# Scan of a hybrid decoder layer: the first group's sums ahead of the inverse's first step, the gate ahead of the state's sum, the output scale on ScalarE, constants as bias of logarithms

## The reference, cut to what matters

```
# SSD branch, per chunk, 4 groups of 8 heads
y = (decay * C B^T * dt) x  +  (C h) * exp(acum)          # inside the chunk + from the state
h = h * exp(last) + (w x)^T B                             # state
y = rmsnorm_per_group((y + D x) * silu(z)) * w            # gate, then a norm per group
# delta-rule branch, per chunk, 8 heads
u, w = (I + A)^-1 [beta v, beta k exp(g)]                 # triangular solve
v_new = u - w S;  o = q S + attn v_new;  S = S exp(last) + k^T v_new
o = rmsnorm(o) * w * silu(gate)
# q and k are l2-normalised: q * rsqrt(sum(q*q) + EPS), and the norms add EPS too
```

## Time and profile before

| what | us |
|---|---|
| median of 3 runs (3299.76 to 3300.80) | 3299.77 |
| the profiled execution | 3298.78 |
| its span in the profile | 3296.9 |
| PE busy, whole span | 2961.9 (90%) |
| DVE busy | 1542.7 (47%) |
| ACT busy | 1008.8 (31%) |
| POOL busy | 387.1 (12%) |

### The profile page before, as it was taken

The page is one execution under the profiler, slowest core; times in us unless marked ns, Lnnn a source line. Parts: engine busy times, 40 slices in busy tenths (PEclk is TensorE's granted clock), DMA queues, the critical chain, the costliest instruction groups (busy, mean ns, idle before and its releaser), DMA issues. The chain is left out here.

```text
span 3296.9 us, 52404 instructions
## 1 busy us (share of the span) xinstructions
PE 2961.9 (90%) x18908; PEld 2803.8 (85%) x18908; DVE 1542.7 (47%) x2327; ACT 1008.8 (31%) x2050; POOL 387.1 (12%) x540
## 2 busy tenths in 40 slices
PE   3799999999999888888888785999879999997998
PEld 2799999999999876777777634999879999997998
DVE  5355555521111177777778654455453323233443
ACT  2222222221121153444444334333341212122332
POOL 2000000000000033222223211000110000000100
PEclk7899999999999999899989886999999999998999
DMA  2222222222242213342222636564531122215443
GB/s 77 80 93 92 91 91 91 91 99 94 93 133 94 94 24 77 86 90 64 64 64 66 168 106 256 176 206 158 171 99 65 58 78 83 78 58 188 169 143 112
DMA packets 238754, 348.18 MB, mean 106 GB/s; under 512 B 154520, under 2 KB 173288, under 8 KB 238368
## 3 DMA queue, kind: packets, MB, share of 16 engines
q1 hardware_dynamic: 233264, 325.20, 31.2%
q0 software_dynamic: 5360, 21.29, 1.8%
HBM read 253.24 MB, written 93.22 MB: 105 GB/s over the span
## 5 line engine op out<-in xcount | busy, mean ns | idle before, releaser
L534 PE MATMUL pps<-h_hi,pwh 128*128 128x352 f32 (+1 forms) x2112 | 689.8, 327 | 16.0 <-DVE pwl L599 16.0
L534 PE MATMUL pps<-h_hi,pwl 128*128 128x352 f32 (+1 forms) x2112 | 686.8, 325 | 0.0
L534 PE MATMUL pps<-h_lo,pwh 128*128 128x352 f32 (+1 forms) x2112 | 685.0, 324 | 0.0
L534 PEld LDWEIGHTS pps<-h_hi,pwh 128*128 128x128 f32 x2112 | 397.4, 188 | 16.4 <-issue 16.4
L534 PEld LDWEIGHTS pps<-h_lo,pwh 128*128 128x128 f32 x2112 | 398.2, 189 | 0.0
L534 PEld LDWEIGHTS pps<-h_hi,pwl 128*128 128x128 f32 x2112 | 397.9, 188 | 0.0
L2299 PE MATMUL u_ps<-f_hi,up_wh 128*128 128x352 f32 (+1 forms) x1056 | 346.0, 328 | 9.4 <-DVE up_wl L2291 9.4
L2299 PE MATMUL u_ps<-f_lo,up_wh 128*128 128x352 f32 (+1 forms) x1056 | 345.0, 327 | 0.0
L2299 PE MATMUL u_ps<-f_hi,up_wl 128*128 128x352 f32 (+1 forms) x1056 | 345.0, 327 | 0.0
L599 DVE TENSOR_TENSOR pwl<-pw,pwh 128x1024 fp32r<-128x1024 f32 x88 | 107.8, 1226 | 505.3 <-ACT pwh L547 498.4
L2299 PE MATMUL merge_ps<-merge_yh,merge_wh 128*128 128x352 f32 (+1 forms) x576 | 190.7, 331 | 34.5 <-DVE merge_yl L2445 27.1
(11 more groups left out here) (457 smaller groups left out, 5198.6 us busy)
## 6 DMA issues: line engine op xcount, KB each, us to landing
projected<-pO SPq DMA_DIRECT2D x88, 536.0 KB, 2.9
pw<-in_w_in SPq DMA_DIRECT2D x88, 512.0 KB, 3.8
merge_w<-in_w_out SPq DMA_DIRECT2D x72, 512.0 KB, 3.4
down_w<-in_w_down SPq DMA_DIRECT2D x48, 704.0 KB, 4.0
up_w<-in_w_up SPq DMA_DIRECT2D x44, 512.0 KB, 4.7
chunk<-projected SPq DMA_DIRECT2D x5, 3744.0 KB, 16.8
scan_chunk<-projected SPq DMA_DIRECT2D x5, 3744.0 KB, 16.4
wo_w<-in_w_o SPq DMA_DIRECT2D x24, 512.0 KB, 3.4
```

The lines of the kernel that those rows point to most:

```text
L534: ins = pe.matmul(ps[:, 3 * u + n, 0:cn], l[u][:, k, :], r[:, k, c0:c0 + cn], start=(k == 0 and a == 0), stop=(k == KD - 1 and a == 2))
```

## The change

Four edits, all in the scan.

1. The order around level 0. On PE the transposes of `mat` come ahead of `turn_out`; group 1's decays come next, then `ssd_gate(0)` (z's transposes) and `ssd_state(0)`; the wait for `v_yg` moves from ahead of level 0 to its third pair. On DVE group 0's scaling and inside sum stand ahead of the first subtractions from D, and `gate_out` between the two kinds of them.
2. In every group DVE gates `y` (`v_yz`) ahead of the state's sum (`v_h1`).
3. The output scale: `normalise` becomes `out_factor` (DVE, the small product alone, now right behind `ssd_weights(0)`), and ACT's `out_scale` writes `on` by eight copies, one per head, with a scale per partition; `turn_out` waits for `a_on`.
4. EPS comes in as the bias of the logarithms (a tile `eps`, set once), and the mean's 1/512 as their scale. L1280, L1298 and L1437 fall away on DVE, and L1276 becomes a copy.

The core of the diff:

```diff
 # PE
-                if not first:
-                    pe.wait_ge(v_on.sem, v_on.ahead(r))
-                    pe.wait_ge(v_qk.sem, v_qk.at(r))
-                    turn_out(r - 1)
                 for hb in range(2):
                     ...
                     transpose_bank(pe, ps[:, B[hb], :], [mat[0:c, 0, 2 * hb + n, :] for n in range(2)], c, ident).then_inc(m_T.sem, 1)
-                ssd_rest(0)
-                pe.wait_ge(v_yg.sem, v_yg.ahead(r))
+                if not first:
+                    pe.wait_ge(a_on.sem, a_on.ahead(r))
+                    pe.wait_ge(v_qk.sem, v_qk.at(r))
+                    turn_out(r - 1)
+                ssd_decays(1, 0)
+                ssd_decays(1, 1)
+                ssd_gate(0)
+                ssd_state(0)
 ...
+                        if l == 0 and pair == 2:
+                            pe.wait_ge(v_yg.sem, v_yg.ahead(r))
 ...
                     if l < 3:
                         ssd_inside(g)
-                        ssd_rest(g)
+                        ssd_gate(g)
+                        if g < 3:
+                            ssd_decays(g + 1, 0)
+                            ssd_decays(g + 1, 1)
+                        ssd_state(g)
 # ACT
             def out_scale(r):
-                act.wait_ge(v_oms.sem, v_oms.at(r))
-                act.activation(lg[0:c, 2, :], ss[0:c, 2, :], ACT.Ln).then_inc(a_oln.sem, 1)
+                act.wait_ge(v_oqs.sem, v_oqs.at(r))
+                act.activation(lg[0:c, 2, :], be[0:c, 3, :], ACT.Ln, bias=eps[0:c, 0:1]).then_inc(a_oln.sem, 1)
                 act.wait_ge(a_oln.sem, a_oln.at(r))
                 act.activation(ors[0:c, :], lg[0:c, 2, :], ACT.Exp, scale=-0.5).then_inc(a_ors.sem, 1)
+                act.wait_ge(v_oq.sem, v_oq.at(r))
+                act.wait_ge(v_o2.sem, v_o2.at(r))
+                for hd in range(HG):
+                    ins = act.activation(on[0:c, hd, :], o[0:c, hd, :], ACT.Copy, scale=be[0:c, 4, hd:hd + 1])
+                ins.then_inc(a_on.sem, 1)
 ...
-                act.wait_ge(v_yms.sem, v_yms.at(r))
-                act.activation(yss[0:c, 2, :], yss[0:c, 1, :], ACT.Ln).then_inc(a_yln.sem, 1)
+                act.wait_ge(a_ysq.sem, a_ysq.at(r))
+                act.activation(yss[0:c, 2, :], yss[0:c, 0, :], ACT.Ln, bias=eps[0:c, 0:1], scale=1.0 / XG).then_inc(a_yln.sem, 1)
 # DVE
-                dve.wait_ge(v_oqs.sem, v_oqs.at(r))
-                dve.tensor_scalar(ss[0:c, 2, :], be[0:c, 3, :], EPS, None, ALU.add).then_inc(v_oms.sem, 1)
 ...
-                dve.wait_ge(v_oq.sem, v_oq.at(r))
-                dve.wait_ge(v_o2.sem, v_o2.at(r))
-                dve.tensor_tensor(on[0:c, :, :], o[0:c, :, :], bcast(be[0:c, 4, :], P), ALU.mult).then_inc(v_on.sem, 1)
 ...
-                dve.wait_ge(a_ysq.sem, a_ysq.at(r))
-                dve.tensor_scalar(yss[0:c, 1, :], yss[0:c, 0, :], 1.0 / XG, EPS, ALU.mult, ALU.add).then_inc(v_yms.sem, 1)
```

More of the change, by code:

```diff
@@ L1104, in _ @@
             chunks(pe, body)
-            pe.wait_ge(v_on.sem, v_on.at(last_round))
+            pe.wait_ge(a_on.sem, a_on.at(last_round))
             pe.wait_ge(v_o2.sem, v_o2.at(last_round))
@@ L1111, in _ @@
             prime(act, a_sdec, a_qsq, a_ksq, a_B, a_cb, a_ln, a_rs, a_dec, a_ysq, a_yln, a_yrs, a_x, a_yn, a_osq, a_oln,
-                  a_ors, a_k, a_kT, a_kbT, a_X, a_vn, a_decL, a_id, a_R)
+                  a_ors, a_on, a_k, a_kT, a_kbT, a_X, a_vn, a_decL, a_id, a_R)
             act.preload_act_table_set("natural_log_exp_and_others")
@@ L1134, in kq_log @@
                 act.wait_ge(v_ss.sem, v_ss.at(r))
-                act.activation(lg[0:c, 0:2, :], ss[0:c, 0:2, :], ACT.Ln).then_inc(a_ln.sem, 1)
+                act.activation(lg[0:c, 0:2, :], ss[0:c, 0:2, :], ACT.Ln, bias=eps[0:c, 0:1]).then_inc(a_ln.sem, 1)
             def kq_scale(u, r):
@@ L1259, in _ @@
             prime(dve, zeroed, v_wg, v_tmp, v_y1, v_h0, v_y2, v_h1, v_yz, v_xdt, v_vb, v_ss,
-                  v_kss, v_kn, v_kbn, v_AT, v_C, v_D1, v_D2, v_qk, v_T, v_TTn, v_yms, v_res, v_o1, v_S0, v_o2,
-                  v_S1, v_rq, v_oqs, v_oq, v_oss, v_oms, v_on, v_ys, v_yg)
+                  v_kn, v_kbn, v_AT, v_C, v_D1, v_D2, v_qk, v_T, v_TTn, v_res, v_o1, v_S0, v_o2,
+                  v_S1, v_rq, v_oqs, v_oq, v_oss, v_ys, v_yg)
             dve.memset(ss[:, :, :], 1.0)
+            dve.memset(eps[:, :], EPS)
             dve.memset(D[:, :, :, :, :], 0.0)
@@ L1275, in kq_sizes @@
                 dve.wait_ge(m_qss.sem, m_qss.at(r))
[L1276 removed]
+                dve.tensor_copy(ss[0:c, 1, :], ps[0:c, E_[2], 0:HG]).then_inc(v_ss.sem, 1)
                 dve.wait_ge(a_ksq.sem, a_ksq.at(r))
[L1278 to L1280 removed]
+                dve.tensor_reduce(ss[0:c, 0, :], sqr[0:c, :, :], AX, ALU.add).then_inc(v_ss.sem, 1)
             def scale_k(u, r):
@@ L1296, in mean_square, with out_factor @@
                                          op0=ALU.mult, op1=ALU.mult).then_inc(v_oqs.sem, 1)
-                dve.wait_ge(v_oqs.sem, v_oqs.at(r))
-                dve.tensor_scalar(ss[0:c, 2, :], be[0:c, 3, :], EPS, None, ALU.add).then_inc(v_oms.sem, 1)
-            def normalise(r, u):
+            def out_factor(r, u):
                 dve.wait_ge(a_ors.sem, a_ors.at(r))
@@ L1380, in body @@
                 ssd_weights(0)
+                if not first:
+                    out_factor(r - 1, 1 - u)
                 for hb in range(2):
@@ L1395, in body @@
                                               ALU.mult).then_inc(v_qk.sem, 1)
-                if not first:
-                    normalise(r - 1, 1 - u)
+                ssd_inter_scale(0)
+                ssd_inside_add(0)
                 dve.wait_ge(a_id.sem, a_id.at(r))
@@ L1402, in body @@
                         "p (h m j) -> p h m j", h=2, j=2), ALU.subtract).then_inc(v_D1.sem, 1)
+                if not first:
+                    gate_out(r - 1, 1 - u)
                 for hb in range(2):
@@ L1406, in body @@
                         "p h (m j) -> p h m j", j=2), ALU.subtract).then_inc(v_D2.sem, 1)
-                if not first:
-                    gate_out(r - 1, 1 - u)
-                ssd_group(0)
+                ssd_inter_add(0)
+                ssd_gate(0)
+                ssd_state_decay(0)
                 ssd_weights(1)
+                ssd_state_add(0)
                 for l in range(nl):
@@ L1440, in body @@
                     dve.wait_ge(v_vb.sem, v_vb.at(r))
-                    dve.wait_ge(v_kss.sem, v_kss.at(r if last else r + 1))
+                    dve.wait_ge(v_ss.sem, v_ss.at(r if last else r + 1))
                     for n in range(NHB):
@@ L1476, in _ @@
             mean_square(last_round)
-            normalise(last_round, last_place)
+            out_factor(last_round, last_place)
             gate_out(last_round, last_place)
```

37 lines of the change are left out of this document (23 added, 14 removed).

## The result

The changed kernel takes 3238.86 us, the median of four runs (3236.23 to 3241.46), against 3299.77 before: a ratio of 0.9821, with a 95% interval of 0.9803 to 0.9839. It is 61 us faster; 3234 was predicted. The profiled execution took 3238.62, 60.2 less than the one of before.

The account below looks back on a forecast made before the run. Bound: a chain PE, DVE, PE in which DVE's order decides. Load 48.1 + L1437 14.0 + ends 10.4 - clock 6.6 = 65.9 us off 3298.78: 3232.9, as median 3234; range 3213 to 3256.

Parts of the forecast that it names:

- The pause ahead of z: Round 4, PE's 3.24 us wait for `tmp` ahead of z's transposes: gone, with 2.2 us or less idle there.
- The load takes over: At `k_in`, rounds 1 to 8: load lands 24.24 us after `gate_out`, so PE newly waits about 1.9 us.
- The first rival: At `k_in`: the load does not bind, all rounds keep 7.5 us; 3215 us, chance 0.10.
- L1437: DVE instruction ahead of `res`: its removal saves PE 1.4 us a round, 14.0 in all (bounds 0 and 15.4).
- The clock: Behind the new pause at `k_in`: half clock costs 1.65 us in four of eight rounds, 6.6 lost (bounds 0 and 26).
- The rival of 26 us: Behind each new pause at `k_in`: the clock falls longer, 26 us lost instead of 6.6; 3253 us, chance 0.14.
- the one of half clock to the round's end: From `k_in` to the next round: half clock loses 12 us in each of eight rounds; 3323 us, chance 0.04.
- Rounds 0, 9 and the end: Round 0 gains 3.9 us, round 9 gains 7.5, uncovered copies after the last round lose 1.0: together 10.4.
- The sum: All terms, in the scan: 48.1 + 14.0 + 10.4 - 6.6 = 65.9 us gained.
- the load's term: Rounds 1 to 8, ahead of `k_in`: 29.5 us of spare time plus 18.6 from earlier `gate_out`, 48.1 gained.
- some 14 us were named as a sign: Rounds 3 and 4 of the scan: together some 14 us shorter, a listed sign that the prediction holds.
- What was said of level 0: Round 4: level 0's products end at 1455.43, `ssd_inter(1)` starts at 1456.0 instead of 1462.53, 6.5 us earlier.

Follow-up runs that it names:

- e1: Changed kernel, chunk load split: first 48 of 72 tiles asked for once QS is done, ahead of the store; 3225.35 us (of two), ratio 0.9789.
- e3: Changed kernel with the state's sum again ahead of gating y in levels 0 to 2; 3235.40 us, ratio 0.9820.
- e6: Changed kernel, load split: first 48 tiles asked for only after the next round's transposes of kb, still ahead of `gate_out`; 3214.51 us, ratio 0.9736.
- e8: Kernel before the change, with the load split and asked for as in e6 and nothing else; 3301.05 us, ratio 0.9993.
- e2: Changed kernel with ten added matmuls of 416 columns on PE ahead of `k_in`, filling the pause; 3228.82 us, ratio 0.9800.
- e9: Changed kernel with group 0's scaling and inside sum on DVE again behind both kinds of subtraction and `gate_out`; 3229.13 us, ratio 0.9793.

## Why the prediction was right

- *The pause ahead of z goes, and `gate_out` moves forward.* As said: 0.18 us left, `gate_out` 3.23 after qk where 3.2 was forecast.
- *The load takes over.* Forecast 24.24 us from `gate_out` to landing and a pause of about 1.9; measured 24.85 and 1.90 to 2.53, in rounds 1 to 8 alone. From the start of x's products (VectorE's) to `k_in` the eight rounds gained 5.15, 4.65, 7.09, 4.92, 7.11, 4.61, 8.45 and 4.58: 46.6, where 48.1 was the term. e1, e3, e6 and e8 show that it is the load, and that it was not before. The first rival (the load doesn't bind, 3215) falls; its time is what e6 reaches by taking the load away.
- *L1437.* 14.0 was too much: PE's wait for `res` fell by 10.3, 1.03 a round, since a hand-over of 0.5 stays and not 0.14.
- *The clock.* It came in six rounds of eight, not in four. From `k_in` to the next start of x's products the eight rounds were to gain 11.2 by L1437 and lose 6.6; together they lost 0.1. With 8.2 for L1437 (eight times 1.03) the clock took 8.3, 1.4 each; by e2 it is 9.5, 1.6 each. So the price of 1.65 was right and the count wrong. That the price was right is luck in part: it was got by halving with the length of the pause, and no such proportion shows here, since the longest pause (2.53, round 6) has no half clock behind it and the shortest (1.90, round 7) has. The rival of 26 us and the one of half clock to the round's end fall.
- *Rounds 0, 9 and the end.* With their share of L1437 13.2 was forecast, 11.45 came (4.30 in round 0, 7.15 from round 9 on).
- *The sum.* Forecast 65.9; the parts measured add up to 58.0 (46.6 - 0.1 + 11.45). The 7.9 that are missing: 1.5 in the load's term, 3.0 from L1437 in rounds 1 to 8, 1.7 by the clock, 1.7 at the ends. All are sizes; no step failed. The whole kernel came 2 us closer to the forecast than its scan did, by luck: the stage behind the scan, the same code, took 141.1 us instead of 143.3. Rounds 3 and 4 together, where some 14 us were named as a sign, are 12.8 shorter.
- *What was said of level 0 was too smooth.* The working has `ssd_inter(1)` start 0.6 behind level 0's products, the list of signs has it wait for nothing; it waits 1.25 a round. Most of the difference is the addition of `tmp` to y: from its start to the gate's it was counted at 0.60 and took 1.16 (1432.88 to 1434.04). It took 1.05 itself beside GpSimd's masks, and 0.69 in e9, where it ran between them. The Trainium skill (SBUF — State Buffer, Who interferes with whom, on the shared port pair) has the rule that a VectorE instruction with two inputs in SBUF and a GpSimd instruction that reads SBUF exclude each other; these two numbers agree with it. L1298, which the prediction names as a second sign of it, reads a single tile and is no example of the rule as it is quoted. As forecast, the wait for the load covered the wait at `ssd_inter(1)`.

What the prediction did not see is how the parts stand to each other. It priced them as a whole, and rightly. Taken one by one, two parts (the gate ahead of the state's sum, the early sums of group 0) are worth 10 to 12 and 8 to 10 us where the load is out of the way. In the changed kernel as it stands, undoing either makes the scan 6 us shorter, and the whole kernel no slower (e3) or 9 to 10 us faster (e9): the waits that come back lie where the load is under way anyway, and the pause at `k_in`, with the half clock behind it, shrinks or goes.

## What to carry to other kernels

When a stall is removed, look for the chain that was late by less: here a load asked for behind the last store had 3 to 5 us to spare, and it took the rest of the gain. Split such a transfer by what its buffer still holds, and ask for the part that is free earlier; that was worth 24 us more than the change (e6). Keep it clear of the loop's turn: just ahead of the turn it gave 18.6 us of the scan (e1), behind it 26.3. Parts that share a bound must be measured without it as well as with it, or good ones look useless.

## What the runs showed of the hardware

After the idle stretch of 1.9 to 2.5 us at `k_in` PE's granted clock fell from the higher level (2.4 GHz) to the lower (1.2 GHz) in six cases of eight; with the same idle time spread in waits of 1.3 us and less (e3) it fell behind none of the eight, and PE's busy time was 6.9 us shorter.

The turn of a hardware loop cost PE 2.5 us, and 5.3 while a 2.5 MB load kept the DMA engines over 90% busy (e1); asked for 14 us after the stop had begun, the same load left it at 2.5 (e6). The branch of the turn ended 1.3 to 1.5 us after a 16 KB packet of the profile's `instruction` queue, which started 1.0 us into the branch without the load and 3.5 to 3.9 us into it beside the load.

The stage behind the scan is the same code in all kernels, and took 141.1 us in the changed kernel and 149.2 in e3, the first row and the second:

```profile
1815.52:1956.60 141.08, 116.62 (x594) 69.83 (x594) 84.55 (x114) 60.52 (x162) 31.99 (x23) 0.75 0.46 161
```

```profile
1806.90:1956.10 149.20, 123.24 (x594) 73.40 (x594) 84.38 (x114) 60.47 (x162) 32.01 (x23) 0.72 0.43 152
```

PE's busy time there is 6.6 us longer at a lower mean clock. Why it falls differently is open: no run was made on it.
